# Odd mixer of a three-block model: q and k norms under the input projection, v token-major, attention by head pairs

## The reference

```python
proj = h @ odd_w_in                      # 512 x 2048
q, k, v, u = jnp.split(proj, 4, axis=-1) # 512 channels each
# attention: 8 heads of 64, chunks of 64 tokens, 8 chunks back
q = rmsnorm(q per head, q_gain); k = rmsnorm(k per head, k_gain)
scores = q @ k.T * 64 ** -0.5 + rel_bias[h, clip(i - j, -128, 128) + 128]
scores = where(key chunk <= query chunk, scores, -inf)
y_c = softmax(scores) @ v
# pooling: 4 groups of 128 channels, windows of 2, 4, 8, 16 tokens
y_d = (trailing_mean(u) - u) @ w_pool[g] * scale
x = x + concat(y_c, y_d) @ odd_w_out
```

## Time and profile before

| what | value |
|---|---|
| median of 3 runs | 3274.4 us |
| lowest, highest | 3270.32, 3275.35 us |
| the profiled execution, its own time | 3276.05 us |
| its span, first to last instruction | 3274.3 us |
| TensorE's mean granted clock | 0.933 of full speed |
| TensorE, VectorE, ScalarE, GpSimd busy | 3100.9, 1470.4, 958.7, 195.8 us |
| odd mixer from its input stage to the output projection | about 1479 to 1768 us of the span |

### The profile page before, as it was taken

One profiled execution on the slowest core, in us unless ns is written; L12 is line 12 of the kernel. 1 busy time (PEld: TensorE's weight loads), 2 busy tenths in 40 slices (PEclk: granted clock), 3 DMA queues, 4 the chain that ended last, 5 costly groups with the idle time before them and its releaser, 6 DMA issues. The chain is left out here.

```text
span 3274.3 us, 34803 instructions
## 1 busy us (share of the span) xinstructions
PE 3100.9 (95%) x12909; PEld 2418.5 (74%) x12924; DVE 1470.4 (45%) x1902; ACT 958.7 (29%) x1276; POOL 195.8 (6%) x211
## 2 busy tenths in 40 slices
PE   6999998789999999999999999999999999889997
PEld 5777876468888788887556888877776777568885
DVE  5574355564443444433223544327873334443323
ACT  4422232233332333221112333222223333233222
POOL 3000040010000000010200000000000000100000
PEclk9999997689999999999557999999998899989998
DMA  3334262123332233323001323334420013223321
GB/s 129 109 120 156 82 186 66 48 74 103 96 110 90 82 96 96 106 68 133 0 1 39 97 96 103 110 104 125 132 64 1 1 58 103 71 79 99 103 100 43
DMA packets 82850, 284.69 MB, mean 87 GB/s; under 512 B 14760, under 2 KB 15400, under 8 KB 82000
## 3 DMA queue, kind: packets, MB, share of 16 engines
q1 hardware_dynamic: 71392, 250.63, 24.0%
q0 software_dynamic: 6768, 26.70, 2.6%
q10 hardware_dynamic: 4608, 6.30, 0.7%
HBM read 262.35 MB, written 14.94 MB: 85 GB/s over the span
## 5 line engine op out<-in xcount | busy, mean ns | idle before, releaser
L177 DVE TENSOR_TENSOR wl<-raw,wh 128x1024 fp32r<-128x1024 f32 (+2 forms) x440 | 573.7, 1305 | 1047.8 <-ACT wh L171 1037.2
L200 PE MATMUL PS<-Hh,wl 128*128 128x512 f32 x2360 | 928.0, 393 | 40.9 <-DVE wl L177 18.0
L201 PE MATMUL PS<-Hh,wh 128*128 128x512 f32 x2360 | 921.3, 390 | 0.0
L202 PE MATMUL PS<-Hl,wh 128*128 128x512 f32 x2360 | 921.2, 390 | 0.0
L171 ACT ACTIVATE wh<-raw 128x1024 fp32r<-128x1024 f32 (+2 forms) x440 | 480.2, 1091 | 1147.6 <-PE PS L202 1030.8
L200 PEld LDWEIGHTS PS<-Hh,wl 128*128 128x128 f32 x2360 | 444.8, 188 | 149.4 <-issue 34.8
L202 PEld LDWEIGHTS PS<-Hl,wh 128*128 128x128 f32 x2360 | 444.7, 188 | 93.2
L201 PEld LDWEIGHTS PS<-Hh,wh 128*128 128x128 f32 x2360 | 445.0, 189 | 92.3 <-issue 1.0
L202 PE MATMUL PS<-ffn_gl,wh 128*128 128x512 f32 x880 | 351.0, 399 | 0.0
L200 PE MATMUL PS<-ffn_gh,wl 128*128 128x512 f32 x880 | 346.7, 394 | 2.6 <-DVE wl L177 2.6
L201 PE MATMUL PS<-ffn_gh,wh 128*128 128x512 f32 x880 | 347.1, 394 | 0.0
(11 more groups left out here) (401 smaller groups left out, 2884.3 us busy)
## 6 DMA issues: line engine op xcount, KB each, us to landing
raw<-in_gu SPq DMA_DIRECT2D x220, 512.0 KB, 3.5
raw<-in_dn SPq DMA_DIRECT2D x80, 704.0 KB, 4.0
raw<-in_hin SPq DMA_DIRECT2D x44, 512.0 KB, 3.8
raw<-in_oin SPq DMA_DIRECT2D x16, 512.0 KB, 3.6
raw<-in_hin_gate SPq DMA_DIRECT2D x16, 512.0 KB, 3.5
X<-QKV ACTq DMA_DIRECT2D x96, 64.0 KB, 2.9
kept_x<-X POOLq DMA_DIRECT2D x16, 256.0 KB, 3.6
raw<-in_eout SPq DMA_DIRECT2D x8, 512.0 KB, 3.6
```

What stands on the lines that cost most here:

```text
L177: self.nc.vector.tensor_sub(self.wl[j % SPLIT][:, 0:kw], self.raw[j][:, 0:kw], self.wh[j % SPLIT][:, 0:kw].bitcast(F32)).then_inc(self.lo_ ...
L200: self.nc.tensor.matmul(out, wl, xh[:, u.k0 + k, :], start=first, stop=False)
L201: self.nc.tensor.matmul(out, wh, xh[:, u.k0 + k, :], start=False, stop=False)
L202: done = self.nc.tensor.matmul(out, wh, xl[:, u.k0 + k, :], start=False, stop=last)
```

## The change

Stages 1 to 4 become two.

`odd_input` is the input projection with the order u, q, k, v. VectorE reads u (i = 0) and q and k (i = 1, 2) out of PSUM, scaled by RS. For each chunk k of q and k, ScalarE squares it, TensorE sums the squares per head with one 128x128 product of 512 columns (`heads`), which lands spread over the partitions; VectorE scales it out of PSUM, ScalarE takes the root, VectorE takes the reciprocal over 128x512 and multiplies q or k by gain and reciprocal. The steps follow the units: the sum of chunk k comes after unit k + 5 in TensorE's queue (`total`), scaling and norm one and two reads later in VectorE's. The v part (i = 3) is token-major: activations are the stationary operand, weights the moving one of 512 columns, with four units adding up in four banks (`token_unit`); ScalarE copies the four banks to V, scaled by a column of RS which TensorE has made by four one-column products. The GpSimd pooling windows run in this stage, after all loads and as u arrives. The bias, with the mask in it, is loaded as a table of 128 by 8 by 512.

`chunk_attend` makes 16 steps, each one query tile of two heads (s = 0, 1). The scores of the two heads lie on partitions 0 to 63 and 64 to 127 of the operands and go to two banks. VectorE adds the table to the scores and takes the maximum in one instruction (`tensor_tensor_reduce`) into SBUF; ScalarE makes the exponentials in place there. Negation and reciprocal are done for both heads at once. The value products of the two heads alternate and go to the lower and upper 64 partitions of one bank. The pooling products and their scaling and splits stand in the last two iterations of the same loop. The flip matrix, the mask row and the head selector are gone; the q scale 64 ** -0.5 is in the root's input.

```diff
+        def token_unit(i, j):
+            tokens, bank, lag = st.tokens[i]
+            xh, xl = st.units[j].x
+            pe.wait_ge(self.lo_ready, st.base + j + 1 + RAW * i)
+            for kk in range(2):
+                wh, wl = (t[j % SPLIT][:, kk * S:(kk + 1) * S] for t in (self.wh, self.wl))
+                k = 2 * j + kk
+                for t in range(TT):
+                    if k == 0:
+                        pe.wait_ge(bank_free, after + st.chunks * (i - lag) + t + 1)
+                    out, sel = self.PS[:, bank + t, :], tokens(t)
+                    self.nc.tensor.matmul(out, xh[:, k, sel], wl, start=k == 0, stop=False)
+                    self.nc.tensor.matmul(out, xh[:, k, sel], wh, start=False, stop=False)
+                    done = self.nc.tensor.matmul(out, xl[:, k, sel], wh, start=False, stop=k == DC - 1)
+            done.then_inc(self.unit_done, 1)
...
+def odd_input(co, st, QK, V, UU, windows, cols, loads):
...
+            def total(n):
+                if n == 3:
+                    for t in range(TT):
+                        m = nc.tensor.matmul(co.PS[:, 6, t:t + 1], co.RS[:, t * P:(t + 1) * P], co.ident[:, 0:1],
+                                             start=True, stop=True)
+                    m.then_inc(spread, 1)
+                if 5 <= n <= 12:
+                    k = n - 5
+                    pe.wait_ge(squared, k + 1)
+                    if k >= 2:
+                        pe.wait_ge(scaled, k - 1)
+                    nc.tensor.matmul(co.PS[:, 4 + k % 2, :], co.heads, SQ[:, k % 2, :], start=True,
+                                     stop=True).then_inc(summed, 1)
+            co.multiply(pe, st, bank_free, between=total)
...
+            def scale(k):
+
+                dve.wait_ge(summed, k + 1)
+                if k >= 2:
+                    dve.wait_ge(normed, k - 1)
+                of_q = k < 4
+                v.tensor_scalar(R[:, k % 2, :], co.PS[:, 4 + k % 2, :], 1.0 if of_q else 1.0 / HD,
+                                HD * EPS if of_q else EPS, ALU.mult, ALU.add).then_inc(scaled, 1)
+
+            def norm(k):
+                dve.wait_ge(rooted, k + 1)
+                v.reciprocal(R[:, k % 2, :], R[:, k % 2, :]).then_inc(inverted, 1)
+                dve.wait_ge(inverted, k + 1)
+                g = cols["q_gain"] if k < 4 else cols["k_gain"]
+                v.scalar_tensor_tensor(QK[:, k, :], QK[:, k, :], co.cols[:, g:g + 1], R[:, k % 2, :],
+                                       ALU.mult, ALU.mult).then_inc(normed, 1)
...
+                    v.tensor_mul(QK[:, k, :], co.PS[:, c, :], co.RS[:]).then_inc(taken, 1)
+                    dve.wait_ge(taken, k + 1)
+                    dve.sem_inc(bank_free, 1)
+                    if k >= 1:
+                        scale(k - 1)
+                    if k >= 2:
+                        norm(k - 2)
+                if i == 3 and c == 0:
+                    norm(6)
+                    scale(7)
+                if i == 3 and c == 1:
+                    norm(7)
...
+def chunk_attend(co, QK, V, BIAS, M, POOLED, PW, cols):
...
+    steps = [(c, t) for c in range(4) for t in range(TT)]
...
+            def scores(k):
+                c, t = steps[k]
+                w = width(k)
+                if k >= 2:
+                    pe.wait_ge(biased, 2 * (k - 2) + 2)
+                for s in range(2):
+                    r = HD * s
+                    nc.tensor.matmul(co.PS[:, 2 * (k % 2) + s, 0:w], QK[r:r + HD, c, t * P:(t + 1) * P],
+                                     QK[r:r + HD, 4 + c, 0:w], start=True, stop=True).then_inc(scored, 1)
...
+                for j in range(t + 1):
+                    for s in range(2):
+                        h = 2 * c + s
+                        m = nc.tensor.matmul(co.PS[HD * s:HD * s + HD, 6 + c % 2, t * P:(t + 1) * P],
+                                             V[:, j, h * HD:(h + 1) * HD], PT[:, k % 2, s, j * P:(j + 1) * P],
+                                             start=j == 0, stop=j == t)
...
+            for k in range(n + 3):
+                if k < n:
+                    scores(k)
+                if 2 <= k < n + 2:
+                    turn(k - 2)
+                if k >= n + 1:
+                    for g in (2 * (k - n - 1), 2 * (k - n - 1) + 1):
+                        pooled_half(g)
+                if k >= 3:
+                    weigh(k - 3)
...
+                        v.tensor_tensor_reduce(SC[:, k % 3, s, 0:w], co.PS[:, 2 * (k % 2) + s, 0:w],
+                                               BIAS[:, 2 * c + s, S - w:S], op0=ALU.add, op1=ALU.max, scale=1.0,
+                                               scalar=NEG, accum_out=ST[:, k % 3, 0, s:s + 1]).then_inc(biased, 1)
```

More of the change, by code:

```diff
@@ L101, in __init__ @@
         self.cols = self.sb("cols", [P, dram["cols"].shape[1]])
[L102 to L103 removed]
+        self.mats = self.sb("mats", [P, 4, P])
+        self.ident, self.triu, self.heads, self.swap = (self.mats[:, k, :] for k in range(4))
         self.M8 = self.sb("M8", [P, S5G])
@@ L1713, in even_mixer, with __init__, pool, step @@
             add_stage(co, st_out, 1.0, gain)
+class Windows:
+    def __init__(self, co, UU, POOLED, PB, RC):
+        self.co, self.UU, self.POOLED, self.PB, self.RC = co, UU, POOLED, PB, RC
+        self.pooling = co.sem("pooling")
+    def pool(self, pool, u_ready):
+        g_ = self.co.nc.gpsimd
+        steps = [0]
+        def step(ins):
+            steps[0] += 1
+            ins.then_inc(self.pooling, 1)
+            pool.wait_ge(self.pooling, steps[0])
+        for g in range(4):
+            pool.wait_ge(u_ready, g + 1)
+            src = self.UU[:, g, :]
+            for k in range(g + 1):
+                d = 1 << k
+                dst = self.POOLED[:, g, :] if (g - k) % 2 == 0 else self.PB[:, 0, :]
+                step(g_.tensor_copy(dst[:, 0:d], src[:, 0:d]))
+                step(g_.tensor_add(dst[:, d:], src[:, d:], src[:, 0:S - d]))
+                src = dst
+            step(g_.tensor_mul(src[:, 0:16], src[:, 0:16], self.RC[:, g, :]))
+            step(g_.tensor_scalar(src[:, 16:], src[:, 16:], 1.0 / (2 << g), None, ALU.mult))
+            step(g_.tensor_sub(src, src, self.UU[:, g, :]))
@@ new lines, in chunk_attend @@
+@stage
+def chunk_attend(co, QK, V, BIAS, M, POOLED, PW, cols):
+    nc = co.nc
+    steps = [(c, t) for c in range(4) for t in range(TT)]
+    n = len(steps)
+    with ExitStack() as ctx:
+        SC = co.sb("ca_sc", [P, 3, 2, S], ctx=ctx)
+        PT = co.sb("ca_pt", [P, 2, 2, S], ctx=ctx)
+        ST = co.sb("ca_st", [P, 3, 4, 2], ctx=ctx)
+        T = co.sb("ca_t", [P, 2, S], ctx=ctx)
+        (scored, biased, negated, powered, inverted, normed, turned, copied, weighted, out_hi, out_lo, pooled, scaled,
+         rounded, parted) = (co.sem(f"ca_{s}") for s in (
+            "scored", "biased", "negated", "powered", "inverted", "normed", "turned", "copied", "weighted", "out_hi",
+            "out_lo", "pooled", "scaled", "rounded", "parted"))
+        block = ctx.enter_context(nc.Block())
+        width = lambda k: (steps[k][1] + 1) * P
@@ new lines, in _ @@
+        @block.scalar
+        def _(act):
+            for k in range(n + 3):
+                if k < n:
+                    w = width(k)
+                    act.wait_ge(negated, k + 1)
+                    for s in range(2):
+                        nc.scalar.activation(SC[:, k % 3, s, 0:w], SC[:, k % 3, s, 0:w], ACT.Exp,
+                                             bias=ST[:, k % 3, 1, s:s + 1], accum_out=ST[:, k % 3, 2, s:s + 1]).then_inc(powered, 1)
+                if 2 <= k < n + 2:
+                    w = width(k - 2)
+                    if k >= 4:
+                        act.wait_ge(weighted, k - 3)
+                    for s in range(2):
+                        act.wait_ge(turned, 2 * (k - 2) + s + 1)
+                        nc.scalar.activation(PT[:, k % 2, s, 0:w], co.PS[:, 4 + s, 0:w], ACT.Copy).then_inc(copied, 1)
+                if k >= n + 1:
+                    for g in (2 * (k - n - 1), 2 * (k - n - 1) + 1):
+                        act.wait_ge(scaled, g + 1)
+                        nc.scalar.activation(M[0][:, 4 + g, :], T[:, g % 2, :], ACT.Copy).then_inc(rounded, 1)
+                if k >= 3 and steps[k - 3][1] == TT - 1:
+                    c = steps[k - 3][0]
+                    act.wait_ge(weighted, k - 2)
+                    nc.scalar.activation(M[0][:, c, :], co.PS[:, 6 + c % 2, :], ACT.Copy).then_inc(out_hi, 1)
```

269 lines of the change are left out of this document (141 added, 128 removed).

## The result

The median fell from 3273.5 us (3270.32 to 3275.35, 4 runs) to 3135.05 us (3130.76 to 3137.49, 4 runs): a ratio of 0.9577, 95% interval 0.956 to 0.9593. The forecast was 3156.5 us; the time lies 21.4 us under it and 1 us under the low end of the range. The profiled execution took 3135.28 us, 140.8 less than the one of before, where the working gave 117.8.

A forecast was written before the change was run, and what follows sets the result against it. TensorE was taken to bound the kernel, by its work and clock. Terms 16 + 4.2 + 76 + 0.65 = 96.9 us replace 214.7, so 117.8 us less: 3156.5 us, range 3136 to 3184.

The forecast's parts named there:

- What bounds, and the sign: Whole kernel: TensorE bounds it by its work and its clock; faster by more than 0.2% had chance 0.97.
- (1) Input stage: Input projection grows by 16 us (12 to 20): 7.2 sums of squares, 1.3 one-column products, 4.5 VectorE lateness, 3 GpSimd contention.
- (2) Boundary: Between input stage and attention: ScalarE's split and four scaled copies of v take 4.2 us; the norms stage goes.
- (3) Attention: Attention with pooling takes 76 us: 65 at upper clock, 105 at lower, mean clock 0.86, 3 more for the start.
- Each product by itself: Attention: TensorE's products counted without overlap between heads, 56 us at the upper clock.
- rival B: Attention: two heads run at once on the array, TensorE 40 us, stage 60 to 62, kernel 3143; chance 0.34.
- The clock of the hybrid: Attention: mean clock as in the hybrid mixer's attention, 0.86, expected from longer unbroken runs of transposes and value products.
- The chain: Attention: transposes wait for copies queued behind exponentials, 1.3 to 2 us four times, 2.5 to fill, 2 to 3 to drain.
- main case: Whole kernel: the prediction's own sum, no head overlap and the hybrid's clock, 3156.5 us (3147 to 3172); chance 0.42.
- C: Attention: clock stays at its lower level, stage 105 us, kernel 3186; chance 0.11.
- D: Attention and input stage: VectorE becomes the bound, fused operation at half rate, more GpSimd contention, kernel 3168; chance 0.10.
- E: Whole kernel: slower than before, needing a fused operation in attention of some 16 ns a column; chance 0.02.

The follow-up runs named there:

- bias_on_tensor: Changed kernel with the bias table added on TensorE by a product with the identity, VectorE only taking the maximum: 3162.02 us, ratio 0.9653.
- copies_first: Changed kernel with ScalarE's two copies of step k - 2 queued ahead of the two exponentials of step k in attention: 3122.65 us, ratio 0.9528.
- no_reciprocal: Changed kernel without the reciprocal of the head norms, q and k multiplied by the root itself: 3124.76 us, ratio 0.9531.
- no_overlap: Changed kernel with both heads' scores from the same rows and both heads' values accumulated in the same half of the bank: 3134.79 us, ratio 0.957.
- heads_apart_again: Changed kernel with both heads' scores from the same rows and value products issued head after head, second profile: 3148.84 us, ratio 0.9603.

## Why the prediction was right and where it was wrong

**What bounds, and the sign.** Right. TensorE was busy 202.3 of the 214.7 us of the old stretch, at a mean clock of 0.54, and the stretch lost work and has a higher clock. Of the gain only the 25 us of bias_on_tensor were isolated by a run.

**(1) Input stage, 16 us, measured 11.85.** TensorE's part was 8.5; 7.6 was measured, and 6.7 in the stage's length, since 0.9 us of waits that the old stage had were filled. VectorE's lateness 4.5, measured 5.1: the sum of its operations against TensorE's unit was the right way to see it. Contention 3, measured 0 (its lower bound). In the trace the stretched split of 1.51 us stands behind a wait of VectorE of 1.65 us; no run tells whether that is so for every stretched operation.

**(2) Boundary.** 4.2, measured 3.8. The four copies took 2.40 us.

**(3) Attention, 76 us and 0.65 to the output projection, measured 63.8: the step that failed.** The term was 12.85 us too large. Three statements stood in it.
*Each product by itself.* This is the step that was wrong in kind. Products that differ in row group (scores) or column group (values) start 6 to 7 ns apart in the trace of copies_first, and two cost what one does: 1.13 against 1.98 us for the scores, 1.09 against 1.96 for eight values. "TensorE: Matmul & The Clock Gate", Part 3 (packing small matmuls), of the Trainium skill says that such products run concurrently, with starts a few ns apart; the traces agree for float32, for rows and for columns. (The Trainium skill names no type for these figures; that they were "measured on other types", as the prediction says, does not stand there.) With the overlap TensorE is busy 39.8 us at a clock of 0.96 (copies_first) where 56 was counted and 40 stood in rival B.
*The clock of the hybrid, 0.86.* The three profiles of the changed kernel had 0.74, 0.81 and 0.74, the same attention in no_reciprocal 0.91, no_overlap 0.88. The forecast looked for the cause in the runs of one kind of product. No run confirms that, and none names another cause: the clock of this stage is not a number that its code fixes.
*The chain.* Right in kind and place: waits of 1.3 to 2 us, one for each pair of heads, by copies queued behind exponentials; measured 1.6 to 2.0, with smaller ones 9.2 us in all. Its size in the sum was wrong: 56 + 4 x 1.3 to 2 + 2.5 + 2 to 3 gives 66 to 69.5 us, where the prediction wrote 65.

How much of the 12.85 us is each? Without any overlap the stage took 68.2 us where the forecast's own conditions gave 76.65. So 8.4 us stay when the failed premise is made true again: the main case was priced too high. 3 us of that were added for the start on top of a mean clock that held the lower level already. By 0.88, that is the lower level in 24% of the time, the forecast's two prices give 1/(0.76/65 + 0.24/105) = 71.5, with the 0.65 us 72.2, and 4.0 us are left as too dear, among them the waits for copies (3.9 us in no_overlap, 5 to 8 counted). The other 4.4 us would be the overlap, net of what waits and clock take back. That is less than the 8 us by which the same attention code differs between profiles, and the totals of the two kernels don't differ either. So the overlap is shown in the array, and its share in this miss is not: the split is an estimate from one profile of no_overlap.

**Rival B** named the right mechanism and a length, 60 to 62 us, that five of the six profiles of this attention come near (60.7 to 63.9; the sixth 55.6). The length is in part luck. B took it from VectorE's 45 us and ScalarE's work in a chain, "whatever the clock does". The same work of the two (37.0 and 36.1 us, measured) in another order of ScalarE's queue gives 46.5 us, and the same order at a clock of 0.91 gave 55.6. C (lower clock throughout), D (VectorE the bound, a fused operation at half rate) and E did not come: the fused operation takes 0.54 us on average with its read-out.

**What the forecast left out.** 5.6 us came outside the changed stages. Ahead of them 1.8 us, with the same code; the start of the input stage lies anywhere from 1473.0 to 1485.4 us in the kernels of the table, so this is scatter. Behind them 3.8: the hybrid attention took 190.4 us at 0.85 before and 185.0 at 0.88 after. In the nineteen profiles of kernels with the change or an edit of it that same code took 183.0 to 193.6 us at 0.89 to 0.83; the three of the changed kernel alone show 185.0, 184.8 and 190.4. So these 3.8 us are where the clock happened to change, and not an effect of the change.

The median forecast missed by 21.4 us: 12.9 in attention, 4.2 in the input stage, 0.4 at the boundary, 5.6 elsewhere less 1.5 between medians and profiles. That the time lies just outside the range, and not inside it, is no more than the scatter; most of the 21 us is the attention term.

## What to carry to other kernels

A stage's clock need not be fixed by its code: six profiles of the same attention gave 55.6 to 63.9 us at 0.91 to 0.74. Take several before a difference of a few us is read. Work that an overlap saves is not yet time saved while TensorE waits for another engine's queue, and a change that only closes such a wait (one queue's order) can give more than the wait: 5 us of waits less, 9 to 17 us of stage. Two float32 products in distinct row or column groups cost one; look at neighbours in the queue, also across loops, since an order head after head still overlaps by half. To say that a mechanism made the time, remove it wholly and look at the kernel's time, with enough runs to see the effect, and not at the record lengths alone.

## What the runs showed of the hardware that was not expected

- Products in distinct groups overlap in float32 too: starts 6 to 7 ns apart at clock 1.00, for two row groups (64 rows each, 512 columns) and two column groups (64 columns each).
- 48 products of no use (11 us at the upper clock) left a 64 us stage as long as it was, one profile each: the mean clock was 0.95 against 0.74. Without them the same attention has also stood at 0.91.
- In heads_apart_again the granted clock stood at 0.50 from 1575 to 1610 us while TensorE was busy 6.9 to 7.0 us in each 7.
- The Trainium skill, "TensorE: Matmul & The Clock Gate", Part 1 (the HAM clock gate), says that the time at which the clock rises varies from run to run. The traces agree that it is not fixed: the three profiles of the changed kernel have 60.7 to 63.8 us and 0.81 to 0.74 in the same stage, and 184.8 to 190.4 us in the same hybrid attention.
- The add with maximum (`tensor_tensor_reduce`, out of PSUM with an SBUF table) takes 0.69 us at 512 columns, 0.42 at 256 and 0.28 at 128, with 0.08 for the read-out of the maximum: at 512 columns no more than one product out of PSUM.
